# PEER gates: indirect accumulating word transfers into a cleared matrix in memory in place of one-hot matrix products

## The reference

```python
v1, i1 = lax.top_k(s1, 16); v2, i2 = lax.top_k(s2, 16)      # 8 heads, 128 keys a side
cand_s = v1[..., :, None] + v2[..., None, :]
top_s, pos = lax.top_k(cand_s, 16)
idx  = ...                                    # expert number i1*128 + i2, of 16384 experts
gate = softmax(top_s)
act = gelu(einsum('tkd,td->tk', u[ix], hx)) * gx     # 128 chosen experts a token
out = einsum('tk,tkd->td', act, v[ix])
```

## Time and profile before

| | us |
|---|---|
| median of 3 runs | 3869.64 (3868.07 to 3871.07) |
| span of the profiled execution | 3869.2 |
| PE busy | 3827.2 (99%) |
| DVE, ACT, POOL busy | 2802.9, 1883.7, 1665.4 |
| DMA, mean over the span | 226 GB/s |

### The profile page before, as it was taken

How to read it: one execution, slowest core, us unless ns; L and a number is a source line. 1 busy time by engine, 2 the same in 40 slices (tenths; PEclk the granted TensorE clock), 3 DMA queues, 4 the chain that set the end, 5 groups by cost and what they waited for, 6 DMA issues and landing times.

```text
span 3869.2 us, 60328 instructions
## 1 busy us (share of the span) xinstructions
PE 3827.2 (99%) x18945; PEld 3308.0 (85%) x18945; DVE 2802.9 (72%) x5195; ACT 1883.7 (49%) x3598; POOL 1665.4 (43%) x1768
## 2 busy tenths in 40 slices
PE   9999999999999999999999999999999999999998
PEld 7665888888888999999788888888888888999997
DVE  4647799778742688887777773999777723888876
ACT  3747433578743333334555553333777723333334
POOL 0311345778730566661200001436887701666641
PEclk9999999999999999999999999999999999999999
DMA  8547566555556899994578773334555566999972
GB/s 276 167 149 196 166 201 204 189 201 196 191 207 201 290 366 361 366 354 153 174 236 244 234 211 108 118 119 142 215 190 189 204 215 206 353 360 366 362 281 93
DMA packets 547287, 875.95 MB, mean 226 GB/s; under 512 B 40592, under 2 KB 384784, under 8 KB 543280
## 3 DMA queue, kind: packets, MB, share of 16 engines
q1 hardware_dynamic: 458688, 605.81, 48.0%
q0 software_dynamic: 51568, 201.04, 14.3%
q10 hardware_dynamic: 36864, 67.13, 4.7%
HBM read 745.57 MB, written 262.21 MB: 260 GB/s over the span
## 4 chain that ended last, share of the span: by engine, by line
PE 91%; ACT 3%; issue 2%; DVE 2%; POOL 1%; DMA 1%; ACTq 0%; DVEq 0%; SPq 0%; POOLq 0%
PE ps L191 83%; PE ps L1771 2%; ACT first_scaled L1790 1%; POOL w_lo L176 1%; PE ps L2314 1%; PE ps L2335 1%; PE ps L1272 1%; PE ps L2085 1%; ACT w_hi L163 1%; PE ps L614 0%; PE ps L615 0%; DMA xbc<-gates 0%; PE ps L600 0%; DVE gate_group L1700 0%; DVE ssd_weights L1122 0%
## 5 line engine op out<-in xcount | busy, mean ns | idle before, releaser
L163 ACT ACTIVATE w_hi<-w_raw 128x1024 fp32r<-128x1024 f32 x692 | 732.7, 1059 | 1194.3 <-PE ps L191 1041.1
L169 DVE TENSOR_TENSOR w_lo<-w_raw,w_hi 128x1024 fp32r<-128x1024 f32 x584 | 718.3, 1230 | 647.7 <-ACT w_hi L163 637.3
L191 PE MATMUL ps<-h_hi,w_hi 128*128 128x512 f32 (+1 forms) x3072 | 1154.1, 376 | 7.7 <-POOL w_lo L176 3.0
L191 PE MATMUL ps<-h_hi,w_lo 128*128 128x512 f32 (+1 forms) x3072 | 1142.1, 372 | 0.0
L191 PE MATMUL ps<-h_lo,w_hi 128*128 128x512 f32 (+1 forms) x3072 | 1141.0, 371 | 0.0
L191 PE MATMUL ps<-y_hi,w_hi 128*128 128x512 f32 (+1 forms) x2368 | 870.0, 367 | 2.0 <-POOL w_lo L176 1.7
L191 PE MATMUL ps<-y_hi,w_lo 128*128 128x512 f32 (+1 forms) x2368 | 867.3, 366 | 0.0
L191 PE MATMUL ps<-y_lo,w_hi 128*128 128x512 f32 (+1 forms) x2368 | 866.9, 366 | 0.0
L191 PEld LDWEIGHTS ps<-h_hi,w_hi 128*128 128x128 f32 x3072 | 577.3, 188 | 97.8 <-issue 11.0
L191 PEld LDWEIGHTS ps<-h_hi,w_lo 128*128 128x128 f32 x3072 | 577.0, 188 | 82.3
L191 PEld LDWEIGHTS ps<-h_lo,w_hi 128*128 128x128 f32 x3072 | 577.5, 188 | 78.0 <-issue 2.1
(11 more groups left out here) (374 smaller groups left out, 3558.3 us busy)
## 6 DMA issues: line engine op xcount, KB each, us to landing
value_rows<-in_v SPq DMA_DIRECT2D x256, 512.0 KB, 6.0
w_raw<-in_u SPq DMA_DIRECT2D x256, 512.0 KB, 3.6
w_raw<-in_v SPq DMA_DIRECT2D x256, 512.0 KB, 5.6
acts<-gelu ACTq DMA_DIRECT2D x256, 256.0 KB, 2.2
gates<-gate_group POOLq DMA_DIRECT2D x28, 2048.0 KB, 8.0
blocks<-acts SPq DMA_DIRECT2D x256, 192.0 KB, 5.2
blocks<-gates SPq DMA_DIRECT2D x96, 512.0 KB, 7.0
w_raw<-in_od_in SPq DMA_DIRECT2D x65, 512.0 KB, 3.6
```

The source lines that it names most:

```text
L163: self.nc.scalar.activation(self.wh[:, slot % SPL, :], self.raw[:, slot, :], ACT.Copy).then_inc(self.sig("w_hi_ready").sem, 1)
L169: self.nc.vector.tensor_tensor(self.wl[:, slot % SPL, :], self.raw[:, slot, :], self.wh[:, slot % SPL, :].bitcast(F32), ALU.subtract).then ...
L191: ins = self.nc.tensor.matmul(out, a[:, s, w], b[:, k, :], start=first and j == 0 and m == 0, stop=last and j == n - 1 and m == 2)
```

## The change

The gate matrix is made in memory by transfers. A new tensor `gate_matrix` for each layer (second key x first key x token, 25 MB) is cleared by 24 stores of 1 MB that SP issues in the loop of TopK. At the end of Decode DVE works out each selection's word address from its two keys and its token, with no transposes. In the stage Scatter, which takes the place of Gates, POOL issues 384 indirect transfers (8 heads x 3 token tiles x 16 selections): each adds 128 gates, one word of each partition's token, at 128 addresses in memory. Before a head's 16 transfers of a tile POOL waits for those of the head before to have landed. PE, ACT and DVE only do the 60 units there. In Values SP waits at tail unit 24, between two weight loads, for all 384 transfers; the gates of a block are then fetched as two 768 KB pieces of 6 KB rows in place of three 512 KB pieces of 1 KB rows, and block 0 is made in the last four units of the tail.

```diff
+class GateMatrix:
+    TILES = GT // P
+    PIECE = 4
+    WIDE = KEYS * GT
...
+        self.rows = flat.rearrange("(p m) o -> p (m o)", p=P)
...
+    def make_none(self, act):
+        self.p.nc.scalar.activation(self.none[:, :], self.p.incl[:, :], ACT.Copy, scale=0.0
+                                    ).then_inc(self.none_made.sem, 1)
+    def clear(self, sp, at):
+        n = self.PIECE
+        sp.dma_start(self.rows[:, at].rearrange("p (n t) -> p n t", n=n),
+                     self.none[:, :].unsqueeze(1).to_broadcast([P, n, T])).then_inc(self.zeroed.sem, 16)
...
+    def scatter(self, pool, m):
+        h, t, k = self.selection(m)
+        kept = self.kept[t]
+        if h and m % SEL == 0:
+            pool.wait_ge(kept.sem, kept.at(16 * SEL * h))
+        pool.indirect_dma_start(self.flat, bass.IndirectOffsetOnAxis(ap=self.at[:, k:k + 1], axis=0),
+                                self.sum[:, k:k + 1], None, compute_op=ALU.add).then_inc(kept.sem, 16)
...
 class TopK:
...
             p.load(sp, i * 8 + u0 + L + 2 * c, (u0 + L + 2 * c) % RAW, us[i * 4 + c, :, :])
+            m.clear(sp, bass.ds(i * (8 * half) + 2 * c * half, half))
             p.load(sp, i * 8 + u0 + L + 2 * c + 1, (u0 + L + 2 * c + 1) % RAW, self.wq[i * 4 + c + L, :, :])
+            m.clear(sp, bass.ds(i * (8 * half) + (2 * c + 1) * half, half))
...
 class Decode:
...
-        pe.wait_ge(self.dr.sem, self.dr.at(1))
-        for k in range(3):
-            for t in range(GT // P):
-                ins = p.nc.tensor.transpose(p.ps[:, 2 + k, t * P:(t + 1) * P],
-                                            self.key[:, k, t * P:(t + 1) * P], p.ident[:, :])
...
+        link(v.scalar_tensor_tensor(out=where, in0=side[1], scalar=float(KEYS * GT), in1=token, op0=ALU.mult,
+                                    op1=ALU.add))
+        link(v.scalar_tensor_tensor(out=where, in0=side[0], scalar=float(GT), in1=where, op0=ALU.mult,
+                                    op1=ALU.add))
+        link(v.tensor_copy(matrix.at[:, :], matrix.place[:, :]))
+        matrix.take(dve)
...
-class Gates:
+class Scatter:
+    UN = 20
+    NS = 3
+    N = UN * NS
...
     def gpsimd(self, pool):
+        m = self.matrix
+        pool.wait_ge(m.zeroed.sem, m.zeroed.at(16 * m.pieces()))
+        pool.wait_ge(m.taken.sem, m.taken.at(1))
+        for k in range(GT):
+            m.scatter(pool, k)
...
 class Values:
     TAIL = 32
     FETCH_AT = 12
-    PIECES = 3
+    GATES_AT = 24
     QUAD = 4
...
+    def fetch_gates(self, sp, i, s, j, again):
...
+        sp.dma_start(self.gt[:, s, j:j + n, :].rearrange("p j t -> p (j t)"),
+                     self.matrix.rows[:, bass.ds(i * (B * DT) + j * DT, n * DT)]).then_inc(self.bl[s].sem, 16)
...
             if 0 <= k < 2 * B:
                 self.fetch(sp, k // B, k // B, k % B, False)
+            if j == self.GATES_AT:
+                self.matrix.wait_kept(sp)
+            k = j - self.GATES_AT
+            if 0 <= k < 4:
+                self.fetch_gates(sp, k // 2, k // 2, k % 2 * self.QUAD, False)
...
-            if k >= self.TAIL - BLOCK:
-                self.make(dve, 0, 0, k - self.TAIL + BLOCK)
+            if k == self.TAIL - 4:
+                for j in (0, self.QUAD):
+                    self.mult(dve, 0, 0, j)
+            if k >= self.TAIL - 2:
+                self.lo(dve, 0, 0, (k - self.TAIL + 2) * self.QUAD)
```

More of the change, by code:

```diff
@@ L1210, with __init__ @@
     N = 4 * PEER_HEADS + 4
-    def __init__(self, p, layer, b, rows, wq, us, sub, before, hn, nxt, ctx):
+    def __init__(self, p, layer, b, rows, matrix, wq, us, sub, before, hn, nxt, ctx):
         H = PEER_HEADS
+        self.matrix = matrix
         self.layer = layer
@@ L1455, with __init__ @@
     N = 16
-    TURN = 15
-    CLEAR = 8
-    def __init__(self, p, layer, b, rows, own, us, n0, nxt, ctx):
+    def __init__(self, p, layer, b, rows, own, matrix, us, n0, nxt, ctx):
         self.p, self.b, self.rows, self.us, self.n0, self.nxt = p, b, rows, us, n0, nxt
[L1461 to L1464, removed]
+        self.layer, self.own, self.matrix = layer, own, matrix
+        self.gs, self.gx_ = (Mark(p.sig(n), 1) for n in ("gate_shifted", "gate_exp"))
         self.S = PEER_HEADS * SEL
@@ L1487, in tensor @@
         p, n0, u0 = self.p, self.n0, self.u0
[L1489 removed]
+        for j in range(self.N):
             self.rows.multiply(pe, n0 + j, (n0 + j) % 2, u0 + j, (u0 + j) % RAW)
[L1492 to L1501 removed]
     def scalar(self, act):
@@ L1518, in gpsimd @@
             p.split_lo_pool(pool, u0 + j + 1, (u0 + j + 1) % RAW)
[L1519 to L1523, removed]
     def vector(self, dve):
@@ L1554, in vector @@
                                      gsum[:, :].unsqueeze(2).to_broadcast([P, TT * PEER_HEADS, SEL]), ALU.mult))
-        dve.sem_inc(self.dr.sem, 1)
+        where = matrix.place[:, :].rearrange("p (t s) -> p t s", s=S)
+        side = [key[:, k, 0:GT].rearrange("p (t s) -> p t s", s=S) for k in range(2)]
+        token = p.token[:, 0:GT // P].unsqueeze(2).to_broadcast([P, GT // P, S])
+        link(v.scalar_tensor_tensor(out=where, in0=side[1], scalar=float(KEYS * GT), in1=token, op0=ALU.mult,
[4 more added lines that the diff above has]
+        matrix.take(dve)
         mine, own = slice(GT // P * S, TT * S), self.own
@@ new lines, with __init__ @@
+    NS = 3
+    N = UN * NS
+    def __init__(self, p, matrix, rows, us, n0, nxt):
+        self.p, self.matrix, self.rows, self.us, self.n0, self.nxt = p, matrix, rows, us, n0, nxt
+        self.u0 = p.unit
+        p.unit += self.N
+    def vector(self, dve):
+        p, u0 = self.p, self.u0
+        dve.wait_ge(p.sig("w_lo_ready").sem, u0 + 1)
+        for k in range(self.N):
+            p.split_lo(dve, u0 + k + 1, (u0 + k + 1) % RAW)
+    def gpsimd(self, pool):
+        m = self.matrix
[3 more added lines that the diff above has]
+            m.scatter(pool, k)
@@ L1784, in scalar @@
                 p.split_hi(act, g * UN + u, u % RAW, g * (UN // RAW) + u // RAW + 1)
[L1785 to L1793 removed]
+                self.rows.gelu(act, g * UN + n0 + k, g * (UN // 2) + (n0 + k) // 2, (n0 + k) % 2, g * UN + u0 + k)
     def sync(self, sp):
@@ L1865, in sync @@
                 self.rows.wait_stored(sp, self.n0 - 2)
-                for s in range(2):
-                    sp.wait_ge(self.gs.gd[s].sem, self.gs.gd[s].at(16 * (2 * self.gs.NS + 1)))
+                self.matrix.wait_made(sp)
             k = j - self.FETCH_AT
@@ L1962, in scalar @@
             p.split_hi(act, u, u % RAW, u // RAW + 1)
-            if k >= self.TAIL - BLOCK:
-                self.his(act, 0, 0, k - self.TAIL + BLOCK)
+            if k >= self.TAIL - 2:
+                for j in range(4 * (k - self.TAIL + 2), 4 * (k - self.TAIL + 3)):
+                    self.hi(act, 0, 0, j)
             self.rows.gelu(act, n, n // 2, n % 2, self.t0 + k)
@@ L2677, in ffn @@
     n2 = n1 + Decode.N
-    n3 = n2 + Gates.NS * Gates.UN
+    n3 = n2 + Scatter.N
     assert n3 + Values.TAIL == KEYS
@@ L2683, in ffn @@
         with ExitStack() as outer:
-            b["sel"] = p.sb("selected", [P, 4, GT + Gates.TK], ctx=outer)
-            b["gates"] = p.sb("gate_group", [P, 2, KEYS, TG], ctx=outer)
+            matrix = GateMatrix(p, p.gate_matrix[layer], whole, outer)
             with ExitStack() as ctx:
@@ L2690, in ffn @@
                 with ExitStack() as c:
-                    topk = TopK(p, layer, b, rows, wq, us, d[f"sub{layer}"], before, hn, firsts(us[n1:]), c)
+                    topk = TopK(p, layer, b, rows, matrix, wq, us, d[f"sub{layer}"], before, hn, firsts(us[n1:]), c)
                 with ExitStack() as c:
-                    decode = Decode(p, layer, b, rows, own, us, n1, firsts(us[n2:]), c)
-            with ExitStack() as c:
-                gates = Gates(p, b, rows, us, n2, d["gates"], firsts(us[n3:]), c)
+                    decode = Decode(p, layer, b, rows, own, matrix, us, n1, firsts(us[n2:]), c)
+        scatter = Scatter(p, matrix, rows, us, n2, firsts(us[n3:]))
         with ExitStack() as c:
             pairs = ((before.hi, before.lo), hn)
-            values = Values(p, b, rows, own, gates, us, d["gates"], vs, pairs,
+            values = Values(p, rows, own, matrix, us, vs, pairs,
                             [pw_[0, :, :], pw_[1, :, :], gate[0, :, :], gate[1, :, :]], c)
             ple = Ple(p, values, d["emb"][layer], gate, f"norm_ple{layer}", pairs, nxt, c, final, then)
-    return ple.last, (topk, decode, gates, values, ple)
+    return ple.last, (topk, decode, scatter, values, ple)
 def trunk(nc, dram):
@@ L2708, in trunk @@
                                                                   kind="Internal").ap()) for n in range(2)]
+        p.gate_matrix = [nc.dram_tensor(f"gate_matrix{n}", [KEYS * KEYS * GT, 1], F32, kind="Internal").ap() for n in range(2)]
         begin = Start(p, [dram["ev_in"][k, :, :] for k in EV_ORDER[:RAW]])
```

200 lines of the change are left out of this document (48 added, 152 removed).

## The result

The changed kernel takes 4322.3 us (median of 4 runs, 4321.0 to 4323.4) against 3868.9 us on the same chip: a ratio of 1.1167, 95% interval 1.1153 to 1.1181. I forecast 3901 us and a range up to 4210 us. The sign was right; the size lies outside the range.

What follows compares the result with a forecast made beforehand. PE, busy for 99%, was taken to bound the kernel. 3869.2 - 111.4 removed + 2 x 68.5 stall + 2 x 1.7 clock + 3 clearing = 3901.2, forecast 3901 us; range 3812 to 4210 us.

Steps and rivals of the forecast that it cites:

- what the removal wins: Gates on PE: dropping one-hot products, start-up, transposes and the gap around them wins 55.7 us a layer, 111.4 in both.
- the clearing: TopK loop: the clearing stores fit beside layer 1's traffic but slightly exceed layer 0's loop; 3 us, ends 0 and 16.
- POOL's start: End of Decode: POOL starts scattering when its last low part is done, at 718.9 us.
- landing to PE: Values' tail: from landed gates through SP's issue, the gates piece, the load and two splits to PE, 8.9 us.
- the clock after a stall: PE after its stall in Values' tail: a lowered clock costs 1.7 us a stall, ends 0 and 4.
- the wait for the head before: POOL in Scatter: waiting for transfers 32 issues back costs nothing, 44 us against 3.4 us to land.
- The tail's next matmul: PE in layer 0's tail: without a stall, unit 25 would start at 1180.7 us.
- the scatter's price: POOL in Scatter: a scatter costs what an own gather does, 0.94 us plus 0.30 between, one in 1.247 us.
- rival 1: POOL in Scatter: scatters cost more than gathers; 4202 us at 1.6 us each, 4720 at 2.19; chance 28%.
- my upper bound of 2.19: POOL in Scatter: a scatter costs at most two gathers back to back, 2 x 0.94 + 0.30 = 2.19 us.
- the case that I held for likeliest: Scatter stage: 384 scatters at the gather's price, locked by DVE, stall PE 68.5 us a layer; 3901 us, chance 42%.
- The hold: POOL in Scatter: DVE's `w_lo` holds index reads, locking four scatters to a unit, 1.367 us each.

Runs made afterwards that it cites:

- half kernel: The changed kernel with only the scatters of heads 0 to 3, 192 a layer, so half of the gates are missing: ratio 0.9729 to the kernel before.
- Parts 1, 4 and 5: Changed kernel with: 1, the add dropped (ratio 1.2218) or scatters turned into gathers (1.2234); 4, direct adding transfers without indices (3780.9 us); 5, 64 words a scatter (4243.9 us).
- part 1: Two variants of the changed kernel: scatters without the add, ratio 1.2218 to the kernel before; scatters turned round into gathers from the same addresses, 1.2234.

## Why the prediction came out as it did

**Right: what the removal wins.** 55.7 us a layer and 3 us for the clearing are 108 us. The half kernel won 105 (99 to 111).

**Right: the ends of the chain.** POOL's start (719.3 for 718.9), landing to PE (10.4 for 8.9), the clock after a stall (2.6 for 1.7), the clearing (3.5 for 3), the wait for the head before (all of POOL's idle time at L392 is "issue", 0.30 each). Together they are off by some 3 us a layer. The tail's next matmul was due at 1183.2, forecast 1180.7.

**Wrong: the scatter's price.** The step that failed is the gather's price for the scatter: "It occupies POOL for 0.94 us, and 0.30 us lie between two: one in 1.247 us". Measured, it is 1.55 + 0.30: one in 1.857 us. With it 384 take 713 us, and with the held reads 724.6 us from the first issue to the last (719.3 to 1443.9). Put into the prediction's own sum, its other terms unchanged, the last lands at 718.9 + 724.6 + 3.4 = 1446.9, PE resumes at 1455.8, and the stall is 275 us for 68.5: 3869.2 - 111.4 + 2 x 275.1 + 2 x 1.7 + 3 = 4314. So this one term is 413 of the 421 us that were missing. With all terms as measured it is 3869.2 + 2 x (274.0 + 2.6 - 52.4) + 4.3 for layer 1's longer stall = 4322. It was rival 1's mechanism. I gave it 28%, named the add as its cause, bounded it at 2.19 us, and then drew the range at 1.6 us, a point between the bounds for which no row spoke.

Parts 1, 4 and 5 give the price its parts: an indirect word transfer without an add 1.27 us from start to start, an add without indices at most 0.86 (the DMA engines are full), both together 1.86, of which some 0.14 go by each 64 words. So it is neither the add alone nor the indices alone, but the two together; what POOL does in that time no trace shows. The Trainium skill's page Collectives: The Full Stack, section The bandwidth ceiling, which I set beside my upper bound of 2.19, has two read descriptors for the adding transfer of a collective and one for its copy. The runs show an adding transfer to be dearer (0.59 us on POOL, 112 packets), but not by a doubling of POOL's 0.94 us, which is what I had made of it.

**Wrong, though no number of the forecast shows it: the case that I held for likeliest does not exist.** I took it that 384 transfers at the gather's pace would disturb nobody, because the gathers of the kernel before don't. Those come in runs of 13 at most (from 1277.9 to 1296.2), and at 1.52 us from one to the next on average; part 1's trouble starts after 14. At the gather's price the kernel takes 1.22 times as long, not 1.01. The slow add is what keeps the changed kernel at 1.12. By part 1's runs a scatter at the price that I took would have put the time further from the forecast, not nearer; an adding one at that price could not be run.

**The hold.** The mechanism was right: in the changed kernel the scatter at 772.46 takes 2.55 us, and a `w_lo` runs from 772.35 to 773.58. But at the real price it locks nothing. Three scatters take 5.57 us, more than a unit's 5.44, so the reads drift against the `w_lo` and one in six or seven units is held: 0.05 us on average, not 0.12.

## What to carry to other kernels

A transfer of a kind that the trace has not (adding, indirect, of words) is priced by its kind, and here the nearest row of another kind was only a floor: let the range reach to the bound, and ask for one measured transfer before 384 are put on a path. Count what one engine must issue between the earliest start and the latest landing (here 453 us, 238 scatters of 1.9 us), and give it no more than that: with 192 the change won 105 us, with 384 it lost 453. And a pace seen in short bursts says nothing on a run of hundreds.

## What the hardware showed that I had not expected

- Plain indirect word transfers of 128 indices, issued without a pause each 1.27 to 1.33 us, slow PE, ACT and DVE to a crawl after some 14 of them (a matmul each 2.80 us, DMA engines 0.05 busy), and for some 30 us beyond the last. At 1.77 us each they don't, and in eights with a wait for landing (1.55 us each on average) hardly. Adding ones at 1.86 us don't either, nor direct adding ones at 0.86 us, which fill the DMA engines (1.00).
- Adding 128 words costs the DMA queue 143 packets (22656 / 158), 112 more than storing them, at 0.045 us a packet of one engine there, and 0.055 where direct ones fill all 16.
- Two DVE instructions of two inputs, 0.03 us apart, let POOL's index read in between them, if it comes 0.12 us after the start, as the lengths say.
